# Blockwise triangular inverse in a gated-delta layer: transposed 64x64 blocks in the other partition half, both corrections over four quadrants and two banks

## The reference, cut to what matters

```python
L = jnp.where(strict, jnp.einsum('bhncd,bhnsd->bhncs', kb, k) * decay, 0.0)
rhs = jnp.concatenate([v * beta[..., None], kb * jnp.exp(G)[..., None]], axis=-1)
sol = lax.linalg.triangular_solve(L + jnp.eye(CHUNK, dtype=F32), rhs, left_side=True, lower=True)
```

## Time and profile before

| | us |
|---|---|
| median of three runs | 2130.4 |
| the runs | 2129.66, 2130.40, 2130.82 |
| span of the profiled execution, first to last instruction | 2129.5 |
| PE busy in that span | 2075.4 |
| DVE busy | 1495.5 |
| ACT busy | 891.4 |
| POOL busy | 177.8 |

### The profile page before, as it was taken

The page is one execution under the profiler, slowest core; times in us unless marked ns, Lnnn a source line. Parts: engine busy times, 40 slices in busy tenths (PEclk is TensorE's granted clock), DMA queues, the critical chain, the costliest instruction groups (busy, mean ns, idle before and its releaser), DMA issues.

```text
span 2129.5 us, 35611 instructions
## 1 busy us (share of the span) xinstructions
PE 2075.4 (97%) x14377; PEld 1803.5 (85%) x14377; DVE 1495.5 (70%) x1941; ACT 891.4 (42%) x1174; POOL 177.8 (8%) x152
## 2 busy tenths in 40 slices
PE   8999999999999999999899999999989999999999
PEld 8988888798888798888798978887869998778998
DVE  6968754778744677644697684556688887588887
ACT  3244444334444423444323444445554334664332
POOL 6630000000000000000063300000100000100000
PEclk9999999999999999999999999999999999999999
DMA  8512655552555553655464046555325555414552
GB/s 248 178 42 80 201 194 182 174 186 92 198 185 190 160 180 124 205 183 191 142 182 139 3 168 203 192 176 159 99 88 170 178 192 164 138 50 160 195 178 99
DMA packets 267625, 333.81 MB, mean 157 GB/s; under 512 B 20562, under 2 KB 230613, under 8 KB 267493
## 3 DMA queue, kind: packets, MB, share of 16 engines
q1 hardware_dynamic: 267493, 331.93, 48.1%
HBM read 330.84 MB, written 1.05 MB: 156 GB/s over the span
## 4 chain that ended last, share of the span: by engine, by line
PE 82%; DVE 10%; ACT 3%; issue 2%; SPq 1%; DMA 0%; POOL 0%; DVEq 0%; ACTq 0%
PE bank L586 45%; PE bank L554 26%; DVE pj L2187 2%; PE bank L1055 2%; ACT stat L1578 1%; DVE w_lo L2228 1%; DVE w_hi L2226 1%; PE bank L819 1%; PE bank L637 1%; DVE sq L2187 1%; PE bank L911 1%; PE bank L981 1%; PE bank L1136 1%; DVE pj L2181 1%; ACT w_hi L1623 1%
## 5 line engine op out<-in xcount | busy, mean ns | idle before, releaser
L2228 DVE TENSOR_TENSOR w_lo<-ring,w_hi 128x2048 fp32r<-128x2048 f32 (+2 forms) x289 | 615.2, 2131 | 375.4 <-ACT w_hi L1623 373.0
L1623 ACT ACTIVATE w_hi<-ring 128x2048 fp32r<-128x2048 f32 (+1 forms) x220 | 418.8, 1905 | 472.4 <-PE bank L586 287.2
L586 PE MATMUL bank<-w_lo,xh 128*128 128x512 f32 x992 | 267.7, 393 | 0.0
L554 PE MATMUL bank<-xh,w_lo 128*128 128x256 f32 (+2 forms) x1832 | 242.1, 284 | 0.0
L586 PE MATMUL bank<-w_hi,xl 128*128 128x512 f32 x896 | 240.6, 390 | 1.0 <-DVE xl L2177 0.9
L586 PE MATMUL bank<-w_hi,xh 128*128 128x512 f32 x896 | 240.9, 391 | 0.6 <-ACT xh L1578 0.6
L554 PE MATMUL bank<-xh,w_hi 128*128 128x256 f32 x1752 | 238.3, 289 | 0.9 <-DVE pj L2177 0.8
L554 PEld LDWEIGHTS bank<-xh,w_hi 128*128 128x128 f32 x1752 | 223.7, 194 | 10.8 <-issue 5.6
L554 PEld LDWEIGHTS bank<-xh,w_lo 128*128 128x128 f32 (+2 forms) x1832 | 229.0, 191 | 1.1
L554 PE MATMUL bank<-xl,w_hi 128*128 128x256 f32 x1752 | 229.9, 284 | 0.0
L554 PEld LDWEIGHTS bank<-xl,w_hi 128*128 128x128 f32 x1752 | 218.9, 192 | 0.4
(11 more groups left out here) (323 smaller groups left out, 2413.0 us busy)
## 6 DMA issues: line engine op xcount, KB each, us to landing
ring<-in_ffn_w_in_dram SPq DMA_DIRECT2D x264, 512.0 KB, 4.4
ring<-in_ffn_w_down_dram SPq DMA_DIRECT2D x88, 512.0 KB, 4.2
ring<-in_gdn_w_in_dram SPq DMA_DIRECT2D x64, 512.0 KB, 5.0
ring<-in_ffn_w_out_dram SPq DMA_DIRECT2D x44, 512.0 KB, 3.9
ring<-in_w_in_dram SPq DMA_DIRECT2D x40, 512.0 KB, 4.8
ring<-in_hgrn_w_in_dram SPq DMA_DIRECT2D x32, 512.0 KB, 4.6
ring<-in_gla_w_in_dram SPq DMA_DIRECT2D x24, 512.0 KB, 4.6
ring<-in_gdn_w_out_dram SPq DMA_DIRECT2D x16, 512.0 KB, 4.4
```

The source lines that it names most:

```text
L554: m = nc.tensor.matmul(cols, *((wk, xk) if tokens == ALL else (xk, wk)), start=(first and step == 0 and k == 0 and (j % 2 == 0)), stop=(la ...
L586: m = nc.tensor.matmul(bank[:, 0:width], xin[:, k0 + k, rows_of], w[:, k, c * width:(c + 1) * width], start=(first and step == 0 and k == ...
L1623: nc.scalar.activation(taken(high_part(u), u), taken(ring[:, u % RING, :], u), ACT.Copy).then_inc(*act_hi.tick())
L2228: v.tensor_tensor(w_lo[:, u % RING, 0:share], w[:, 0:share], high[:, 0:share], ALU.subtract).then_inc(*dve_lo.tick())
```

## The change

The transposed blocks are kept in the other partition half than the blocks themselves. The first inverse is therefore written crosswise, in two DVE instructions of 64 partitions, where one of 128 stood; the transposing matmuls and the first products of levels 1 to 5 write to the other half than they read, so they use the quadrants (low, high) and (high, low). In a correction the product for X goes across and the one for the transpose stays in its half, so that the two corrections of a pair use all four quadrants; they alternate in the program, and they go into two banks, `z` and `zt`, each claimed on its own. PE waits for the transposed block of the level before, from level 2 on, where it waited only at level 6. DVE subtracts the two corrections in two instructions of 128x256 up to level 4; at level 5 it writes the transposed blocks crosswise, in two instructions as before.

```diff
--- before.py
+++ after.py
@@ -344,6 +344,7 @@
 
         cx = flat(yb)[:, 0:16 * HALF2].rearrange("p (j n) -> p j n", j=16)
         blocks = (slice(0, HALF2), slice(HALF2, HALF))
+        crossed = ((blocks[0], blocks[1]), (blocks[1], blocks[0]))
         xx = flat(inv[:, 0:16, :]).rearrange("p (g two j n) -> p g two j n", g=4, two=2, j=4)
         lb_masked, lb = (flat(ct)[:, 16 * HALF2 * n:16 * HALF2 * (n + 1)].rearrange("p (j n) -> p j n", j=16) for n in range(2))
 
@@ -353,6 +354,7 @@
             return xx[:, j // 4, 0, j % 4, :]
 
         def transposed(j):
+
             return xx[:, j // 4, 1, j % 4, :]
 
         def group(g, which):
@@ -977,8 +979,8 @@
                         for j in range(4 * g, 4 * g + 4):
                             cols_of = slice((j % 4) * HALF2, (j % 4 + 1) * HALF2)
                             if lv < 6:
-                                for r in blocks:
-                                    m = nc.tensor.matmul(b[r, cols_of], lb_masked[r, j, :], inverse(j)[r, :], start=True, stop=True)
+                                for r, to in crossed:
+                                    m = nc.tensor.matmul(b[to, cols_of], lb_masked[r, j, :], inverse(j)[r, :], start=True, stop=True)
                             else:
                                 t0 = (j // 8) * T
                                 m = nc.tensor.matmul(b[HALF2:HALF, cols_of], lt[0:HALF2, j % 8, t0 + HALF2:t0 + HALF], inverse(j)[0:HALF2, :],
@@ -1032,8 +1034,8 @@
                 b = psum.claim(pe, "transposed", layer, g)
                 pe.wait_ge(*dve_gdn.at("XT", layer, 0, g))
                 for j in range(4 * g, 4 * g + 4):
-                    for r in blocks:
-                        m = nc.tensor.matmul(b[r, (j % 4) * HALF2:(j % 4 + 1) * HALF2], transposed(j)[r, :], ident[r, r],
+                    for r, to in crossed:
+                        m = nc.tensor.matmul(b[to, (j % 4) * HALF2:(j % 4 + 1) * HALF2], transposed(j)[r, :], ident[r, r],
                                              start=True, stop=True)
                 m.then_inc(*pe_gdn.tick("transposed", layer, g))
 
@@ -1041,18 +1043,20 @@
 
 
                 b = psum.claim(pe, "z", layer, lv, g)
+                if lv < 6:
+                    bt = psum.claim(pe, "zt", layer, lv, g)
                 pe.wait_ge(*act_gdn.at("cx", layer, lv, g))
-                if lv == 6:
-                    pe.wait_ge(*dve_gdn.at("XT", layer, 5, g))
+                if lv > 1:
+                    pe.wait_ge(*dve_gdn.at("XT", layer, lv - 1, g))
                 for j in range(4 * g, 4 * g + 4):
-                    c = (j % 4) * HALF2
+                    of = slice((j % 4) * HALF2, (j % 4 + 1) * HALF2)
                     if lv == 6:
-                        m = nc.tensor.matmul(b[0:HALF2, c:c + HALF2], cx[HALF2:HALF, j, :], inv[HALF2:HALF, 16 + j, HALF2:HALF],
+                        m = nc.tensor.matmul(b[0:HALF2, of], cx[HALF2:HALF, j, :], inv[HALF2:HALF, 16 + j, HALF2:HALF],
                                              start=True, stop=True)
                         continue
-                    for left, right, c in ((transposed(j), cx[:, j, :], c), (cx[:, j, :], transposed(j), c + T)):
-                        for r in blocks:
-                            m = nc.tensor.matmul(b[r, c:c + HALF2], left[r, :], right[r, :], start=True, stop=True)
+                    for r, to in crossed:
+                        nc.tensor.matmul(b[to, of], transposed(j)[r, :], cx[r, j, :], start=True, stop=True)
+                        m = nc.tensor.matmul(bt[r, of], cx[r, j, :], transposed(j)[r, :], start=True, stop=True)
                 m.then_inc(*pe_gdn.tick("z", layer, lv, g))
 
             def head_norm(layer, g, act_sig, pe_sig, both):
@@ -2656,8 +2660,9 @@
 
                 def first_inverse(g):
                     dve.wait_ge(*pool_gdn.at("masked", layer, 0, g))
-                    tt(s, xx[:, g, 1, :, :], ident64[:, :].rearrange("p (a n) -> p a n", a=1).to_broadcast([P, 4, HALF2]),
-                       lb_masked[:, 4 * g:4 * g + 4, :], ALU.subtract, "XT", layer, 0, g)
+                    for r, to in crossed:
+                        tt(s, xx[to, g, 1, :, :], ident64[r, :].rearrange("p (a n) -> p a n", a=1).to_broadcast([HALF2, 4, HALF2]),
+                           lb_masked[r, 4 * g:4 * g + 4, :], ALU.subtract, "XT", layer, 0, g)
 
                 for h in range(8):
                     dve.wait_ge(*pe_gdn.at("bcast", layer, h))
@@ -2676,14 +2681,16 @@
                 def corrected(lv, g):
                     dve.wait_ge(*pe_gdn.at("z", layer, lv, g))
                     b = psum.bank("z", layer, lv, g)
-                    if lv < 5:
-                        X = xx[:, g, :, :, :].rearrange("p two j n -> p (two j n)")
-                        tt(s, X, X, b[:, :], ALU.subtract, "X", layer, lv, g)
-                    elif lv == 5:
+                    if lv < 6:
+                        bt = psum.bank("zt", layer, lv, g)
                         tt(s, group(g, 0), group(g, 0), b[:, 0:T], ALU.subtract, "X", layer, lv, g)
-                        for r in blocks:
-                            tt(s, inv[r, 16 + 4 * g:16 + 4 * g + 4, r], xx[r, g, 1, :, :],
-                               b[r, T:2 * T].rearrange("p (h n) -> p h n", h=4), ALU.subtract, "XT", layer, lv, g)
+                        if lv < 5:
+                            tt(s, group(g, 1), group(g, 1), bt[:, 0:T], ALU.subtract, "XT", layer, lv, g)
+                        else:
+                            for r, to in crossed:
+                                tt(s, inv[to, 16 + 4 * g:16 + 4 * g + 4, to], xx[r, g, 1, :, :],
+                                   bt[r, 0:T].rearrange("p (h n) -> p h n", h=4), ALU.subtract, "XT", layer, lv, g)
+                        psum.release(s, "zt", layer, lv, g)
                     else:
                         ts(s, inv[0:HALF2, 16 + 4 * g:16 + 4 * g + 4, HALF2:HALF], b[0:HALF2, 0:T].rearrange("p (h n) -> p h n", h=4),
                            -1.0, ALU.mult, None, None, "XT", layer, lv, g)
```

## The result

The changed kernel takes **2134.9 us** (median of ten runs) where the kernel before took 2131.2 beside it: ratio 1.0023, 95% interval 1.0015 to 1.0031. Forecast were 2129.5 us and no change, with a range of 2119 to 2133. Measured again later, beside the kernel before each time, the change came out at 1.0018 (1.0008 to 1.0029) and 1.0026 (1.0017 to 1.0035). It is slower by 0.2%, some 5 us. One run of all that follow, the fourth of e10 (2592 us, granted clock 0.751), was slow and is left out of its ratio and time.

A forecast was written before the change was run, and what follows sets the result against it. PE's pace and instruction fetch were taken to bound the inverse stretches together, the fetch alone after the change. Terms -2.2 + 0.6 + 0.7 = -0.9 us from the 2130.4 us median gave 2129.5 us, range 2119 to 2133.

The forecast's parts named there:

- Part 1: Corrections in four quadrants: PE needs about 4.3 us a level, the fetch alone sets the pace, gain 2.2 us.
- the reading: In the inverse stretches, PE runs one block of 256 instructions while the next is fetched; both limits about 3.7 us.
- the three rivals: Fetch gives way: 2116 us, chance 0.15; pairs only: 2131.7 us, 0.15; quadrants in each other's way: 2168 us, 0.06.
- a turn: Fetching one block of PE instructions in the inverse: 3.85 us taken, halfway between plain 3.7 and the present mean 4.02.
- 13 blocks: Blocks of 256 PE instructions after the first one, mean 4.02 us; each was to give 0.17 us, 2.2 in all.
- The late starts: Instruction packets starting late in several blocks, one block taking 4.49 us; PE's pace was not obviously their cause.
- Parts 2 and 3: More PE waits for second bank and transposed block: 0.6 us; VectorE's subtraction in two instructions: hidden behind PE.
- Part 4: First inverse in two halves of 64 partitions: 0.35 us a layer on the path, 0.7 us in all.
- the two in the scores: Two of the eight lengthened first-inverse instructions, each about 0.35 us longer, before the stretch; mostly hidden under PE's transposes.

The follow-up runs named there:

- e10: Kernel before with two blocks in one 128x128 product with zeros for the transposed correction, ScalarE copying first products in two halves: 2160.1 us, ratio 1.0147.
- e14: Kernel before with ScalarE copying each first product of levels 1 to 5 five times, so that PE waits: 2172.8 us (one run).
- e7: Changed kernel with half the instructions in first products and corrections of levels 1 to 5, same columns, odd heads' own values left out: 2118.9 us, ratio 0.9944.
- e3: Changed kernel with 11 idle products of 128x384 a layer to keep PE busy: ratio 1.0068 to the kernel before.
- e17: Kernel before, two quadrants, with half the instructions of levels 1 to 5, same columns, odd heads' own values left out: 2124.2 us, ratio 0.9972.

## Why the prediction was wrong

**Part 1, the reading and the gain.** The reading held: four passes per 58 ns, the fetch alone setting the pace, gaps at block ends, PE at some 2.9 us a block. The half-instruction pair shows it in reverse: with half the instructions the gaps go, and four quadrants gain. None of the three rivals happened. The term was mis-sized: I took 3.85 us for a turn "halfway", between bounds of 3.4 and 4.1; it is 3.99, so 13 blocks give 0.4 us, not 2.2. The twin without crossing says 0.7 us, with an error of 0.4 and less if the clock's part is overstated. The late starts that I thought of as a share of now's blocks belong to the fetch itself.

**Parts 2 and 3, 0.6 us.** The second bank, its waits and subtractions measured 1.6 us of work (error 0.4), over twice the term.

**Part 4, 0.7 us.** The halves measured 1.5 us of work (error 0.4). The price of one was right: 460 ns in the changed kernel, where the whole took 493. The overlap was wrong. I had let the two in the scores hide under PE's transposes, but the path moves to them. The chain of waits before the second transposes, in the kernel before and then in the changed one:

```profile
135.69 0.22 PE bank L912 x2
135.91 0.64 PE bank L1036 x16
```
```profile
135.89 0.43 DVE inv L2181
...
136.46 0.70 PE bank L1038 x16
```

The first product comes 0.27 us later a layer with the halves alone and 0.52 us with the crossing (2.63, 2.90, 3.15 us behind the first transpose); why the crossing adds to it is open.

**The step that failed outright** is that PE's new idle time was costed at nothing. The forecast named it ("PE's busy time in them down to about 3") and took the granted clock of 1.00 in the earlier trace rows as given, though those rows came from a PE with two short pauses a layer. With pauses at nearly every block the clock falls to 1.2 GHz behind the first layer's inverse in three traces of three, and sometimes elsewhere in the stretch. As far as these runs show, that is an interaction: the passes became cheaper, the fetch turned the saving into idle time, and the idle time lowered the clock of what follows.

The sum, against the kernel before: -0.7 us from the quadrants, +3.5 us from halves and banks, +2.4 us from the clock (16.1 less 13.7), 5.2 us in all. This divides the measured difference of the means, so that it adds up proves nothing; each term has its own experiment. The forecast had -2.2, +1.3 and no third term. Of the 6.1 us between its -0.9 and 5.2, the clock is 2.4, the costs 2.2 and the gain 1.5: had the clock held, the sum would still have been some 3.7 us too low.

What is shown: that the fall behind the first inverse goes with the crossing (three traces of three, none of the seven in two quadrants without added idle time or fillers), that an idle PE brings a fall without crossing (e14, one trace), that crossing without the pauses has none (e7), and that a filled PE has none behind the inverse (e3). What is not: the condition. The quadrant fillers had PE at 3.93 of 6 us before 172 us and the clock stayed at 1.00 in that trace, as it did behind the second inverse in two of the changed kernel's three. The split into clock and work is an estimate too.

The Trainium skill (TensorE: Matmul & The Clock Gate, section "HAM oscillation — how this bites in real kernels") describes PE falling to half speed when it waits for data between bursts of work. The traces agree in kind: 431 ns for a pass that took 281. The waits that the page tells of are longer than any single one here, so it does not say that this change had to bring a fall; but it names the kind of cost that the forecast did not weigh.

## What to carry to other kernels

Where many small matmuls already go at the pace of their instructions, cheaper passes bought next to nothing here; count instructions per product first, and ask what the engine does with the time saved. A pause that costs nothing on the path can still be paid for behind it, by a lower clock in the next dense stretch. What was added for the new layout (halves, a second bank, waits) was the largest sure part of the bill here, 3.5 us.

## What the runs showed of the hardware

- A fetch turn does not shorten when PE takes its instructions faster: 3.99 us a block with four quadrants, 4.02 with two.
- A quadrant's pass costs by the columns it moves: 16 passes of 64 columns in 0.47 us (kernel before), of 128 columns in 0.87 us (chain of e17), both with 64 columns of weights in two quadrants.
- Idle PE time can be paid for behind it: after blocks with PE busy some 2.9 of 4 us the granted clock fell to the 1.2 GHz level for 6.8 us, and products that took 281 ns took 431.
- A whole-array pass of 64 columns with 128 columns of weights takes 130 ns of the chain, where two quadrants finish a pass each 29 ns: putting two blocks into one product with zeros made levels of 9.2 us out of 5.9, some 15 us a layer.
